# Latent attention with the query norm as a row factor of the exponential, and rotary half swaps by DMA

## The reference, cut to what matters

```
# block 1, latent attention: 8 heads of 128 (nope) + 64 (rope)
q = rms_norm(q, q_norm_w)                       # over all 192 of a head
k = rms_norm(concat(k_nope, k_rope), k_norm_w)  # k_rope is shared by the heads
q = concat(q[..., :128], apply_rope(q[..., 128:], pos))
k = concat(k[..., :128], apply_rope(k[..., 128:], pos))
sc = einsum('bqhd,bkhd->bhqk', q, k) * 192 ** -0.5      # masked by chunks of 64
o = softmax(sc) @ v
# block 2, sparse attention: 8 heads of 64
q, k = rope(q), rope(k)
q_idx, k_idx = rope(q_idx), rope(k_idx)         # index heads: 8 of 64, one key
score = sum_h relu(q_idx . k_idx) * w_idx       # causal; the best 128 keys a query are kept
o = softmax(q . k over the kept keys) @ v
```

## Time and profile before

| | us |
|---|---|
| median of 3 runs | 2142.48 |
| the profiled execution | 2142.85 |
| its span | 2141.0 |
| PE busy in the span | 2031.1 (95%) |
| POOL, DVE, ACT busy | 982.3, 909.1, 804.8 |
| mean granted TensorE clock | 0.977 of 2.4 GHz |

### The profile page before, as it was taken

The page is one execution under the profiler, slowest core; times in us unless marked ns, Lnnn a source line. Parts: engine busy times, 40 slices in busy tenths (PEclk is TensorE's granted clock), DMA queues, the critical chain, the costliest instruction groups (busy, mean ns, idle before and its releaser), DMA issues.

```text
span 2141.0 us, 26269 instructions
## 1 busy us (share of the span) xinstructions
PE 2031.1 (95%) x10166; PEld 1639.2 (77%) x10166; DVE 909.1 (42%) x1508; ACT 804.8 (38%) x1057; POOL 982.3 (46%) x766
## 2 busy tenths in 40 slices
PE   6997899999999999999999888989999999999997
PEld 3785896875778887888888576966887788888886
DVE  1679554766433044232200587457944452111101
ACT  3565224346554224222222543343225743222221
POOL 3636613644313464655555373013443265565652
PEclk9998999999999999999999899999999999999999
DMA  6311104721112332222233211011222222222222
GB/s 274 99 60 59 40 1 200 277 79 40 47 53 79 113 123 79 95 92 92 97 117 115 92 60 60 2 50 40 99 79 79 81 98 99 99 99 99 98 99 79
DMA packets 29482, 194.87 MB, mean 91 GB/s; under 512 B 5040, under 2 KB 7216, under 8 KB 8752
## 3 DMA queue, kind: packets, MB, share of 16 engines
q1 hardware_dynamic: 29360, 193.19, 24.8%
HBM read 188.99 MB, written 4.19 MB: 90 GB/s over the span
## 4 chain that ended last, share of the span: by engine, by line
PE 81%; DVE 12%; ACT 3%; DMA 2%; POOL 1%; issue 1%; SPq 0%; ACTq 0%; DVEq 0%; POOLq 0%
PE ps L411 22%; PE ps L412 21%; PE ps L413 21%; PE ps L471 2%; DVE ar L2391 1%; DVE sm L2390 1%; DMA ar<-ada_dram 1%; DVE ar L1844 1%; POOL WL L2476 1%; PE ps L827 1%; PE ps L840 1%; PE ps L501 1%; DVE ar L1870 1%; PE ps L895 1%; DVE ar L1944 1%
## 5 line engine op out<-in xcount | busy, mean ns | idle before, releaser
L2476 POOL TENSOR_TENSOR WL<-raw,WH 128x512 fp32r<-128x512 f32 x588 | 774.1, 1317 | 951.5 <-ACT WH L1278 915.3
L411 PE MATMUL ps<-hH,WH 128*128 128x512 f32 x1648 | 662.1, 402 | 27.9 <-POOL WL L2476 6.6
L413 PE MATMUL ps<-hH,WL 128*128 128x512 f32 x1648 | 648.4, 393 | 0.0
L412 PE MATMUL ps<-arR,WH 128*128 128x512 f32 x1392 | 542.5, 390 | 0.0
L1278 ACT CAST WH<-raw 128x2048 fp32r<-128x2048 f32 x147 | 280.8, 1911 | 503.5 <-DMA raw<-panels_dram 501.9
L411 PEld LDWEIGHTS ps<-hH,WH 128*128 128x128 f32 x1648 | 313.9, 190 | 110.3 <-issue 36.1
L413 PEld LDWEIGHTS ps<-hH,WL 128*128 128x128 f32 x1648 | 313.7, 190 | 67.3
L412 PE MATMUL ps<-xL,WH 128*128 128x512 f32 x848 | 336.6, 397 | 0.0
L412 PEld LDWEIGHTS ps<-arR,WH 128*128 128x128 f32 x1392 | 262.0, 188 | 54.3 <-issue 0.2
L411 PE MATMUL ps<-arR,WH 128*128 128x512 f32 x592 | 230.6, 390 | 1.4 <-DVE ar L1927 1.4
L413 PE MATMUL ps<-arR,WL 128*128 128x512 f32 x592 | 230.3, 389 | 0.0
(11 more groups left out here) (376 smaller groups left out, 2230.2 us busy)
## 6 DMA issues: line engine op xcount, KB each, us to landing
raw<-panels_dram SPq DMA_DIRECT2D x145, 1024.0 KB, 4.8
ar<-ada_dram SPq DMA_DIRECT2D x12, 2048.0 KB, 12.0
xT<-xT_dram SPq DMA_DIRECT2D x2, 2048.0 KB, 9.4
out_dram<-xT SPq DMA_DIRECT2D x8, 512.0 KB, 2.6
xT<-out_dram SPq DMA_DIRECT2D x1, 2048.0 KB, 10.8
wide<-wide_dram SPq DMA_DIRECT2D x1, 1024.0 KB, 6.7
raw<-panels_dram SPq DMA_DIRECT2D x1, 992.0 KB, 5.7
raw<-panels_dram SPq DMA_DIRECT2D x1, 960.0 KB, 6.0
```

The source lines that it names most:

```text
L411: mm(out, lhs[0], rhs[0], start=first, stop=False)
L412: mm(out, lhs[0], rhs[1], start=False, stop=False)
L413: return mm(out, lhs[1], rhs[0], start=False, stop=final)
L2476: ins = tt(WL[:, n % SLOTS, c], raw[:, n % SLOTS, c], WH[:, n % SLOTS, c].bitcast(F32), ALU.subtract)
```

## The change

- The queries are no longer scaled by their norm. The factor is per query and head, so it is a factor of a row of the scores. It is applied as the per-partition scale of the exponential (Q_SCALE, a 128x32 table with 192 ** -0.5 in it), and DVE's negated maximum is multiplied by it. The norm weights of query and key nope parts are multiplied together and put on the keys. ACT puts the rope weight on QR while it copies it from PSUM, and squares it there.
- qss becomes one bank of 8 rows: 12 f32 matmuls of the eight nope squares and the four rope squares by slices of the constant "head_sums" (the constant "rot" is gone), in front of uk, and four small transpositions between uk and mv.
- kss: DVE adds the square of the rotary key to rows 0 to 63 of each head's nope square (k_sq), and one matmul a head is left.
- All rotations on PE (krot, 4 qrot, 5 irot, 8 arot) are gone. SP swaps the halves by DMA from SBUF to SBUF in groups of four DMAs of 32 partitions, at six places of its queue; the sign is in the sine table. DVE multiplies the swapped tile by the sine in SBUF.
- PE does two of the eight aq jobs in front of the index scores. Sparse attention waits for dsa_qk to reach 8.
- One more tile (extra) is allocated.

```diff
-    m["rot"] = np.where(same & (j % 64 == c % 64 + 32), -1.0, 0) + np.where(same & (j % 64 + 32 == c % 64), 1.0, 0)
+    m["head_sums"] = (c == 7) | ((c == 22) & (j < 64)) | ((c == 23) & (j >= 64))
...
-        RS_Q, RS_K = (15, 48, 44, 45), (15, 48, 12, 13)
+        RS_K, QR_SQUARE, KSQ = (15, 48, 12, 13), (10, 15, 48, EXTRA), (14, 49, 10, EXTRA)
+        KRW_SWAP, QR_SWAP, INDEX_SWAP, AQ_SWAP, AK_SWAP = 14, 44, 7, 12, 35
+        Q_LOG, Q_SCALE = 0, 1
...
-                pe.wait_ge(sem("kr_w"), 1)
-                begin("krot")
-                end(mm(pst("krot"), const("rot"), tile(KRW), start=True, stop=True))
                 project("mq", h_mix, 2, i0=8)
                 ada(11)
                 project("mq", h_mix, 2, i0=10)
+                begin("qss")
+                for h in range(H):
+                    pe.wait_ge(sem("nope_sq"), h + 1)
+                    mm(pst("qss")[0:H, :], const("head_sums")[:, 7 - h:15 - h], tile(MV + h), start=(h == 0), stop=False)
+                for p in range(4):
+                    pe.wait_ge(sem("qr_sq"), p + 1)
+                    ins = mm(pst("qss")[0:H, :], const("head_sums")[:, 22 - 2 * p:30 - 2 * p], tile(QR_SQUARE[p]), start=False, stop=(p == 3))
+                end(ins)
...
-                for h in range(H):
-                    column_sums("qss", h, [tile(MV + h // 2), tile(MV + 4 + h % 4)],
...
+                narrow_turn("qss", ("qss", 0), tile(MV + 7), H)
...
-                for p in range(4):
-                    pe.wait_ge(sem("qr_w"), p + 1)
-                    begin("qrot", p)
-                    end(mm(pst("qrot", p), const("rot"), tile(QR + p), start=True, stop=True))
                 for h in range(H):
-                    column_sums("kss", h, [tile(8), tile((14, 49)[h % 2])], [(sem("kr_sq"), 1), (sem("nope_sq"), H + h + 1)],
-                                sel=[const("top64"), const("ones")])
+                    column_sums("kss", h, [tile(KSQ[h % 4])], [(sem("k_sq"), h + 1)])
...
-                for i in (4, 0, 1, 2, 3):
-                    emptied(pe, "ai", i)
-                    begin("irot", i)
-                    end(mm(pst("irot", i), const("rot"), tile(QI + i), start=True, stop=True))
+                project("aq", h_mix, 2)
                 for i in range(24):
                     qt, h = i // 8 + 1, i % 8
                     if qt == 1:
-                        emptied(pe, "irot", h // 2)
+                        pe.wait_ge(sem("index_roped"), h // 2 + 2)
...
-                project("aq", h_mix, 8)
+                project("aq", h_mix, 6, i0=2)
...
-                for i in range(8):
-                    emptied(pe, "aq", i)
-                    begin("arot", i)
-                    end(mm(pst("arot", i), const("rot"), tile(AQ + i), start=True, stop=True))
...
+            def swap_rows(dst, src, n, done):
+                for q in range(4):
+                    here, there = slice(32 * q, 32 * q + 32), slice(32 * (q ^ 1), 32 * (q ^ 1) + 32)
+                    sp.dma_start(ar[there, dst:dst + n, :], ar[here, src:src + n, :]).then_inc(sem(done), 16)
...
+                if (stage, i) == ("ukv", 1):
+                    sp.wait_ge(sem("kr_w"), 1)
+                    swap_rows(KRW_SWAP, KRW, 1, "krw_swapped")
+                if (stage, i) == ("gate_dn0", 0):
+                    for j in range(8, 12):
+                        emptied(sp, "mq", j)
+                    swap_rows(QR_SWAP, QR, 4, "qr_swapped")
+                if (stage, i) == ("aq", 1):
+                    for j in (0, 1, 4):
+                        emptied(sp, "ai", j)
+                    swap_rows(INDEX_SWAP, QI, 2, "index_swapped")
+                    swap_rows(INDEX_SWAP + 4, KI, 1, "index_swapped")
+                if (stage, i) == ("aq", 2):
+                    for j in (2, 3):
+                        emptied(sp, "ai", j)
+                    swap_rows(INDEX_SWAP + 2, QI + 2, 2, "later_index_swapped")
...
...
+                        link(af(tile(QR_SQUARE[i - H]), pst("mq", i), ACT.Square), sem("qr_sq"), i - H + 1)
+                        link(nc.scalar.mul(tile(QN + i), pst("mq", i), col("qn_rope")), *read("mq", i))
...
-                for g in range(2):
-                    rstds("qss", range(4 * g, 4 * g + 4), RS_Q, 1.0 / 192, sem("q_rstd"), sem("q_scaled"))
+                filled(act, "qss_turn")
+                turned = pst("qss_turn")[:, 0:NT * H].rearrange("p (t h) -> p t h", h=H)
+                link(af(sm4[:, Q_LOG, :, 0:H], turned, ACT.Ln, bias=col("eps"), scale=1.0 / 192), *read("qss_turn"))
+                link(af(sm4[:, Q_SCALE, :, 0:H], sm4[:, Q_LOG, :, 0:H], ACT.Exp, bias=st[:, 58:59], scale=-0.5), sem("q_scale"), 1)
...
-            def rope(dst, src, job, i, tmp):
-                filled(dve, job, i)
-                link(tt(tmp, pst(job, i), trig[:, 1, :], ALU.mult), *read(job, i))
-                link(tt(dst, src, trig[:, 0, :], ALU.mult))
-                link(tt(dst, dst, tmp, ALU.add))
+            def rope(x, swapped, s, value):
+                link(tt(tile(swapped), tile(swapped), trig[:, 1, :], ALU.mult))
+                link(tt(tile(x), tile(x), trig[:, 0, :], ALU.mult))
+                link(tt(tile(x), tile(x), tile(swapped), ALU.add), s, value)
...
+                dve.wait_ge(sem("krw_swapped"), 64)
+                rope(KRW, KRW_SWAP, sem("k_rotated"), 1)
+                dve.wait_ge(sem("qr_swapped"), 64)
+                for p in range(4):
+                    rope(QR + p, QR_SWAP + p, sem("q_roped"), p + 1)
...
                 for h in range(H):
-                    dve.wait_ge(sem("q_rstd"), h + 1)
...
+                    dve.wait_ge(sem("nope_sq"), H + h + 1)
+                    sq = tile(KSQ[h % 4])[0:64, :]
+                    link(tt(sq, sq, krope[0:64, :], ALU.add), sem("k_sq"), h + 1)
...
-                    if i >= H + 2:
-                        filled(pool, "kss", i - H - 2)
-                    elif 4 <= i < H:
-                        filled(pool, "qss", i - 4)
+                    if i == H:
+                        pool.wait_ge(sem("k_rotated"), 1)
+                    if i == H + 2:
+                        filled(pool, "qss")
+                    if i >= H + 4:
+                        filled(pool, "kss", i - H - 4)
```

97 lines of the change are left out of this document (57 added, 40 removed).

## The result

The changed kernel takes 2132.38 us (median of 8 runs, 2120.13 to 2137.95) against 2143.32 for the kernel before (8 runs). The ratio is 0.9939 with a 95% interval of 0.9918 to 0.9961: 0.6% faster, 11 us where 25 were forecast, and outside the range of 2112 to 2124. The profiled execution took 2133.09 us, its span is 2131.3, its granted clock 0.970 (before 0.977).

The account below looks back on a forecast made before the run. PE, busy 95% of the span, was taken to bound the kernel. Gains of 10.6 (latent), 7.3 (index) and 7.2 us (aq rotations) sum to 25.1, taking 2142.85 to 2117.7, forecast 2117.4 us as median; range 2112 to 2124.

Parts of the forecast that it names:

- the gap at the key sums: Latent attention, fifth key sum: PE idles 4.9 us for POOL's square behind a split; then the clock falls to half.
- a sign of being wrong: Listed observation that would refute the forecast: PE waiting at the first scores of either attention; no size given.
- the latent stretch: Query and key preparation up to the key sums' end before latent attention: gain 10.6 us, 12.8 with the clock held.
- the sum: Whole kernel: gains of 10.6, 7.3 and 7.2 make 25.1 us, taken from 2142.85; chance 0.62 of 2114 to 2120.
- The query sums: Twelve matmuls with eight output rows, ahead of uk: 0.88 us each, without a gap.
- The third rival: Narrow query-sum matmuls take 0.25 us each, so mv ends 7.5 us earlier; whole time 2110; chance 0.05.
- The exponential: Latent attention: scale by a pointer and row factor on the maximum cost 0 to 0.5 us; taken as 0.
- the index stretch: Block 2, index rotations and scores, with two aq jobs moved ahead: PE through at 1480.3 instead of 1487.6, gain 7.3 us.
- 8 us, the tightest: Time for the second index group's swap to land before four DVE operations for the fifth index head; landing taken as 5 to 7.
- Rival 1: Swap DMAs take near 19 us a group, delaying later index heads by 8 us and latent by 1; 2126; chance 0.14.
- Rival 2: Clock holds through the gap at the key sums, or that gap is shorter: 2.2 us more gained, 2115.2; chance 0.12.
- Rival 4: Swap DMAs make the kernel slower: gain gone from 26 us a group, about 2160 at 35 us; chance 0.02.

Follow-up runs that it names:

- warm_keysum: The changed kernel with six more f32 matmuls in PE's gap ahead of the fifth key sum, results overwritten; 2127.01 us, ratio 0.9932 against the kernel before.

## Why the prediction was wrong

**Right: the direction, and the mechanism of the stretches in the main.** No rotation matmul is left, and the gap at the key sums and its chain are as drawn. Two waits were not drawn: 1.52 us at the adaptation rows, and 0.52 us for ACT at the first latent scores, which the forecast had named as a sign of being wrong.

**Somewhat too large: the latent stretch.** 9.0 us measured against 10.6. Up to mv's end it is 1.2 us less, above all the wait of 1.52 us at the adaptation rows, which was not in the sum at all. The key sums take 14.6 us from mv's end and not 15.4: the gap is 6.18 us and not 4.9, above all since the fifth key sum starts 1.7 us behind the first square's end (508.3), where I took 0.7 for the addition, but the last four take 4.85 us and not 7.0. The fall of the clock behind the gap is there (0.50), but its price is 0.55 us at the sums and nothing at the scores by warm_keysum, where I had put 2.2 us. The end of the key sums before was misread by 0.6 us: 529.35 is the end of the last record, and the next job had started at 528.78. Behind the sums another 0.7 us go, most of it the wait for ACT. So the small miss is partly luck: the gap and the price of its fall were both off, and in opposite directions.

**The query sums.** They took 0.87 us each (24 records from 467.33 to 477.79), with eight output rows as with 128. The third rival, 0.25 us, is refuted.

**The exponential.** I took 0 out of 0 to 0.5; from the first scores to the product behind the attention it is 0.45 us more. ACT's rows show the longer operation, after and before, of the same 128x128 form:

```profile
L1384 ACT ACTIVATE ar<-ar,st,sm 128x128 f32<-128x128 f32 x8 | 4.0, 495 | 0.2
```

```profile
L1358 ACT ACTIVATE ar<-ar,st 128x128 f32<-128x128 f32 x8 | 3.2, 402 | 0.2
```

The pointer costs 93 ns an operation; that the 0.45 us come from it was not tested. The Trainium skill has the same: ScalarE: Activation LUTs, "What ACT_TABLE_LOAD costs", says that each per-partition pointer operand of an ACTIVATE adds about 93 ns; this case's trace agrees.

**Mis-sized: the index stretch.** 4.85 us against 7.3 (12.04 less the 7.2 of the removed arot, which came as forecast). The sentence that failed is "8 us, the tightest": four DVE operations were reckoned at 0.7 us each, and the landing at 5 to 7 us. DVE's program also has the rotations of all five tiles ahead of its first addition, so the late group holds up the adding as a whole and not only the fifth head: it starts at 1475.47, and PE is through 9.6 us later, as forecast (9.7). The group needed 7.8 us, 2.4 of them for four issues in SP's queue, and POOL's split, which the two aq jobs moved beside them, made DVE's operations 1.7 us long. The price is the 2.36 us wait, nearly all of the 2.45 us missing here. Of the Trainium skill's figures (my estimate from SBUF — State Buffer, "Door 1: The DMA port swizzle", was a landing at 1463 to 1466) the trace shows more: 1468.7, for 512 KB in four pieces of 32 partitions, and 6.9 us for one piece of a 1 MB group against 4.8 us for a panel of 1 MB. Half the rate for 32 partitions is not refuted by that, the issues one after another are what the estimate left out. On DVE beside POOL the same page of the Trainium skill says, "Who interferes with whom", that an operation of DVE with two inputs in SBUF and one of GpSimd that reads SBUF contend. The trace agrees: 0.69 us alone, 1.69 beside a split. What speaks against moving rotations from PE to DVE is this price, and only where DVE is waited for.

**Wrong: the sum.** The step that failed is 2142.85 - 25.1. It took for granted that all that the change leaves alone keeps its time: a term put at nothing, without a reason. In the traces it does not: 4.3 us less ahead of the change, 16.0 us more in the recurrence stage. Of the miss of 15 us, 4.5 are terms of the sum (25.1 against 20.6) and some 11 are the time outside the stretches, where the granted clock is the difference that the traces show. Two of the eight runs, 2120.13 and 2123.75 us, had clocks of 0.979 and 0.977 instead of 0.969 to 0.972; they lie near the sum's 2117.4, at 2.7 and 6.4 us above it. No rival named this, and the earlier trace rows had invited it: a gap of 4.7 us with a fall and one of 2.51 us without. What I read there as a length that decides is, in these traces, the moment as well: the same 1.84 us let the clock fall in one trace and not in the other. The Trainium skill says so: TensorE: Matmul & The Clock Gate, "What's actually happening", has the chip's look at TensorE's activity run free, not starting with the kernel, so that one kernel sees its changes of clock at different points in different runs. The stage table agrees, and no run here shows more of it than that.

**The rivals.** Rival 1 (slow swaps) is true in small: 2.4 us in the index stretch, none in the latent one. Rival 2 (the clock holds at the key sums) would have been worth nothing at the first scores, by warm_keysum. Rival 4 did not come near.

**What stays open:** which gap starts the long stretch at half clock, and why the kernel before hardly ever meets it (63 of its 65 runs beside the experiments have a clock of 0.975 or more) while the changed one mostly does (six of its eight have 0.969 to 0.972). The runs show that the same instructions take either time, not what decides it in a given execution.
